# A two-block transformer kernel: queries ahead of keys in latent attention, merge gates and output tiles released earlier

## The chip, the cores and the metric

The kernel runs on one core of one Trainium2 chip. The metric is the device time of one execution in microseconds. Three runs of the kernel before took 3114.63, 3116.35 and 3122.04 us; the median is 3116.35 us.

## What is computed

Two blocks of two layers each work on 256 tokens of width 1024; the first block also has 256 context tokens, which its first layer updates and its second layer only reads. One layer of the first block has, beside norms and modulation, three mixers (latent attention, gated linear attention, neighbourhood attention), a gated merge and a feed-forward part. Cut to what matters here:

```python
def mla_mixer(a_lat, a_ctx, ...):             # latent attention, 8 heads
    qn, qr = mla_queries(a_lat, q_norm_w, w_q_up)      # 64 + 32 features per head
    qr = apply_rope(qr, cos, sin)
    kn, kr, v = mla_keys(a_lat, kv_norm_w, w_kv_up)
    kr = apply_rope(kr, cos, sin)
    ...
    # scores over latent and context keys, softmax, times v

def merge_branches(ya, yb, yc, gates, w_a_o, w_b_o, w_c_o, w_out):
    ga, gb, gc = jnp.split(jax.nn.sigmoid(gates), N_BRANCH, axis=-1)
    return (ga * (ya @ w_a_o) + gb * (yb @ w_b_o) + gc * (yc @ w_c_o)) @ w_out

h = h + g1 * merge_branches(ya, yb, yc, gates, w_a_o, w_b_o, w_c_o, w_out)
```

`gates` is part of the normed input times `w_in`, so it does not depend on the three mixers; `ya`, `yb` and `yc` are their outputs.

## The kernel before, in words

Every product is made of three matmuls (L566 to L568, in `three`): a float32 operand is split into a high part and a low part, and high times high, high times low and low times high are added up in PSUM. Weights come in panels of up to 1 MB. A panel takes this way: SyncE issues its load into one of 3 `raw` buffers (`load_raw`), ScalarE copies it to one of 3 `whi` buffers (L534, in `split_act`, which first waits until the panel three before has been used), VectorE (first five eighths) and GpSimd (the rest) subtract to `wlo` (L543, `split_lo`), and TensorE opens the panel (`open_panel`) when all three are done. When TensorE has used a panel it adds one to `panel_used`. Each engine's program is written out by hand in the order of its instructions, with `step(p)` at the places where it splits the panel two ahead. A stage of the network opens on an engine with `stage(...)` (L574), which waits until all four engines have ended the stage before.

Latent attention (`("mla", l)`, L950 on TensorE). Eight heads; per head `mla_heads` (L1021) projects the keys into bank 7 (6 matmuls of 512 columns) and then the queries into bank 6 (9 matmuls; 512 columns in layer 0, 256 in layer 1, because there the context has no queries). VectorE's `heads` (L2301) waits for both (`qk_done`, L638), scales the keys into `kt` (L2306) and the queries into `qt` (L2307); then TensorE's `mla_rot` (L1043, the matmul L1045) rotates `qt` and VectorE's `rope` (L2271 to L2274) finishes it. GpSimd copies the shared rotary keys `kr` into `kt` (L2752). The next head is prepared at the second item of a head (`prep` on TensorE, `hook` on VectorE); an item is one head and one tile of 128 queries, four a head in layer 0, two in layer 1. Items go through scores (L1064), maximum (L2156), exponential (L1633), transposes (L870), copies (L1644) and the product with the values (L880). In layer 0 the modulation vectors are computed between the items (L770, L759, `mod_vectors` L2042); they share bank 7 with the keys, so TensorE waits for them from head 2 on before it projects a head's keys. The key weights are panel p0 + 5 and the query weights panels p0 + 4 (heads 0 to 3) and p0 + 6 (heads 4 to 7).

Merge (`("merge", l)`, L1322). When the neighbourhood attention has ended, ScalarE copies the 12 tiles of mixer outputs `y` to `yh` (L1870) and VectorE subtracts to `yl` (L2474). TensorE waits for the stage and for the last `yl`, and then loops over 8 output tiles: three gates (24 matmuls each, from `xh`, `xl`, into banks 0 to 2) and three branches (12 matmuls each, from `yh`, `yl`, into banks 3 to 5), from three panels a turn. ScalarE makes the sigmoids (L1880, L1883), VectorE the products and the sum `mf` (L2482 to L2490), which adds one to `merged`. In layer 0 the tiles are 512 columns wide (latent and context tokens), in layer 1 256.

Output (`("out", l)`, L1350). ScalarE waits for all 8 `mf` and for all panels of the merge (L1889), copies `mf` to `xh` (L1891), VectorE subtracts to `xl` (L2497), and TensorE waits for the last `xl` and multiplies with four panels of `w_out`, two tiles of 24 matmuls each (`generic_f`, L822). `three` can also wait for each `xl` by itself, when it is given `fresh`; the norms use this.

Waits of the kernel before that the change touches:

```python
# TensorE, merge, ahead of the loop
stage(pe, "pe", tg, ("na", l))
pe.wait_ge(*dve_done.at((tg, "yl")))
# TensorE, output
stage(pe, "pe", tg, ("merge", l))
pe.wait_ge(*dve_done.at((tg, "ml")))
# ScalarE, output
stage(act, "act", tg, ("merge", l))
act.wait_ge(merged, 8 * (l + 1))
act.wait_ge(panel_used, base[tg])
```

## Time and profile before

| what | value |
|---|---|
| median of the runs | 3116.35 us |
| profiled execution, its own time | 3119.45 us |
| span of its profile | 3117.7 us |
| busy: TensorE, weight loads | 90%, 80% |
| busy: VectorE, ScalarE, GpSimd | 44%, 39%, 36% |
| mean granted clock of TensorE | 0.951 |
| moved by DMA | 413.54 MB, mean 133 GB/s |
| latent attention, heads, layer 0 and 1 | about 124 to 275 us, 1309 to 1390 us |
| merge, layer 0 and 1 | about 598 to 807 us, 1627 to 1742 us |
| output, layer 0 and 1 | about 811 to 860 us, 1745 to 1774 us |

All times in the trace count from the start of the span. A line of the timeline gives start, duration, engine, line of the program, operation, tiles and shape, count of merged instructions, and in brackets how long the engine had been idle before and what released it. In the rows PE is TensorE, DVE VectorE, ACT ScalarE, POOL GpSimd and SPq the queue of SyncE. A clock of 1.00 is 2.4 GHz and one of 0.50 is 1.2 GHz. The duration of one matmul overlaps with the next one, so that the distance of the starts tells the pace.

### The profile page before, as it was taken

To read this page: it belongs to the slowest core of one execution; us is meant where nothing else is said; L and a number is where in the kernel's file an instruction comes from. 1 tells how busy PE (TensorE), PEld (TensorE's weight loads), DVE (VectorE), ACT (ScalarE), POOL (GpSimd) and SP (SyncE) were. 2 spreads that over 40 slices of the span, in tenths; PEclk is the share of its full clock that TensorE was granted. 3 is DMA by queue.
4 is the path that set the end of the run, shared out by engine and by line. 5 is a ranking of instruction groups with operands and counts; after the bars stand their busy time and mean duration, and the time that the engine had idled before them with its cause. 6 is when DMAs were issued, how large, how long until landed. Compare 5 with 4: busy or idle time off the path is not lost. (4 is left out here: it accounts for less than half of the span.)

```text
span 3117.7 us, 52810 instructions
## 1 busy us (share of the span) xinstructions
PE 2812.8 (90%) x20541; PEld 2502.8 (80%) x20541; DVE 1359.5 (44%) x2405; ACT 1217.7 (39%) x1791; POOL 1117.6 (36%) x457
## 2 busy tenths in 40 slices
PE   6789879799889999888789899899889999988998
PEld 4557667588779999566679799899779989977898
DVE  2443533332343433444434543534564353456433
ACT  2322223333244444422345444444444444444443
POOL 0101020132235565111214455354425555632453
PEclk8899989899989999998999999999999999989999
DMA  5454034533336666211415566465225646622563
GB/s 173 131 180 147 14 83 127 156 91 104 94 109 192 188 194 191 83 29 41 88 48 152 164 197 189 141 198 165 95 82 162 188 138 197 190 84 68 149 186 97
DMA packets 570660, 413.54 MB, mean 133 GB/s; under 512 B 36566, under 2 KB 548252, under 8 KB 570524
## 3 DMA queue, kind: packets, MB, share of 16 engines
q1 hardware_dynamic: 570524, 411.69, 44.6%
q8 instruction: 91, 1.49, 0.2%
q14 instruction: 45, 0.37, 0.0%
HBM read 410.58 MB, written 2.88 MB: 133 GB/s over the span
## 5 line engine op out<-in xcount | busy, mean ns | idle before, releaser
L543 POOL TENSOR_TENSOR wlo<-raw,whi 128x768 fp32r<-128x768 f32 (+2 forms) x353 | 1020.3, 2894 | 1701.6 <-ACT whi L534 1701.2
L566 PE MATMUL psum<-xh_n,whi 128*128 128x256 f32 (+1 forms) x3208 | 932.3, 291 | 79.6 <-DVE rtmp L2612 21.7
L567 PE MATMUL psum<-xl_n,whi 128*128 128x256 f32 (+1 forms) x3208 | 915.1, 285 | 0.0
L568 PE MATMUL psum<-xh_n,wlo 128*128 128x256 f32 (+1 forms) x3208 | 914.7, 285 | 0.0
L543 DVE TENSOR_TENSOR wlo<-raw,whi 128x1280 fp32r<-128x1280 f32 (+2 forms) x353 | 531.2, 1505 | 665.3 <-ACT whi L534 665.1
L534 ACT ACTIVATE whi<-raw 128x2048 fp32r<-128x2048 f32 (+2 forms) x353 | 643.2, 1823 | 396.0 <-PE psum L925 171.8
L566 PEld LDWEIGHTS psum<-xh_n,whi 128*128 128x128 f32 x3208 | 615.4, 192 | 114.4 <-issue 57.7
L568 PEld LDWEIGHTS psum<-xh_n,wlo 128*128 128x128 f32 x3208 | 617.3, 192 | 5.5
L567 PEld LDWEIGHTS psum<-xl_n,whi 128*128 128x128 f32 x3208 | 616.4, 192 | 4.7
L923 PE MATMUL psum<-hidh,whi 128*128 128x256 f32 x1232 | 344.0, 279 | 7.0 <-issue 7.0
L925 PE MATMUL psum<-hidh,wlo 128*128 128x256 f32 x1232 | 343.6, 279 | 0.0
L924 PE MATMUL psum<-hidl,whi 128*128 128x256 f32 x1232 | 343.6, 279 | 0.0
L923 PEld LDWEIGHTS psum<-hidh,whi 128*128 128x128 f32 x1232 | 234.1, 190 | 7.5 <-issue 7.5
L925 PEld LDWEIGHTS psum<-hidh,wlo 128*128 128x128 f32 x1232 | 234.7, 191 | 0.0
L924 PEld LDWEIGHTS psum<-hidl,whi 128*128 128x128 f32 x1232 | 234.1, 190 | 0.0
L1653 ACT ACTIVATE sg<-psum 128x256 f32<-128x256 f32 x154 | 59.2, 385 | 420.5 <-PE psum L568 420.4
L2201 DVE TENSOR_TENSOR hidf<-sg,psum 128x256 f32<-128x256 f32 x154 | 64.8, 421 | 259.9 <-ACT sg L1653 259.7
L566 PE MATMUL psum<-xh,whi 128*128 128x512 f32 (+1 forms) x360 | 146.1, 406 | 23.2 <-ACT whi L534 19.9
L567 PE MATMUL psum<-xl,whi 128*128 128x512 f32 (+1 forms) x360 | 143.3, 398 | 0.0
L568 PE MATMUL psum<-xh,wlo 128*128 128x512 f32 (+1 forms) x360 | 142.8, 397 | 0.0
L566 PEld LDWEIGHTS psum<-xh,whi 128*128 128x128 f32 (+1 forms) x360 | 68.9, 191 | 44.5 <-issue 19.0
L2203 DVE TENSOR_TENSOR hidl<-hidf,hidh 128x256 fp32r<-128x256 f32 x154 | 70.6, 458 | 74.6 <-ACT hidh L1655 74.6
(337 smaller groups left out, 3804.3 us busy)
## 6 DMA issues: line engine op xcount, KB each, us to landing
raw<-in_ffn_w_in SPq DMA_DIRECT2D x176, 512.0 KB
raw<-in_w_in SPq DMA_DIRECT2D x136, 512.0 KB
raw<-in_w_ffn_in SPq DMA_DIRECT2D x132, 512.0 KB
raw<-in_w_mod SPq DMA_DIRECT2D x96, 512.0 KB
raw<-in_ffn_w_out SPq DMA_DIRECT2D x88, 512.0 KB
raw<-in_w_ffn_out SPq DMA_DIRECT2D x66, 512.0 KB
raw<-in_w_out SPq DMA_DIRECT2D x32, 512.0 KB
raw<-in_w_a_o SPq DMA_DIRECT2D x16, 256.0 KB
```

Source lines behind the costliest of these rows:

```text
L534: act.activation(whi[slot][:, 0:size], raw[r % 3][:, 0:size], ACT.Copy).then_inc(hi_ready, 1)
L543: eng.tensor_tensor(wlo[slot][:, c0:c1], raw[raw_at[p0] % 3][:, c0:c1], whi[slot][:, c0:c1].bitcast(F32), ALU.subtract).then_inc(sem_, 1)
L566: pe.matmul(dst, sh, mh, start=start and n == 0, stop=False, skip_group_check=True)
L567: pe.matmul(dst, sh, ml, start=False, stop=False, skip_group_check=True)
L568: last = pe.matmul(dst, sl, mh, start=False, stop=n == len(pairs) - 1, skip_group_check=True)
L923: pe.matmul(dst, hi[:, w0:w0 + P], hidh[:, s_, j, :], start=False, stop=False, skip_group_check=True)
L924: pe.matmul(dst, hi[:, w0:w0 + P], hidl[:, s_, j, :], start=False, stop=False, skip_group_check=True)
L925: m = pe.matmul(dst, lo[:, w0:w0 + P], hidh[:, s_, j, :], start=False, stop=False, skip_group_check=True)
L1653: act.activation(sg[:, c, :], bank[4 + c][:, 0:S], ACT.Silu).then_inc(silu_done, 1)
L2201: dve.tensor_tensor(hidf[:, c, :], sg[:, c, :], bank[4 + c][:, S:2 * S], ALU.mult).then_inc(hid_done, 1)
L2203: dve.tensor_tensor(hidl[:, s_, c, :], hidf[:, c, :], hidh[:, s_, c, :].bitcast(F32), ALU.subtract).then_inc(hid_lo, 1)
```

## The change

It makes three edits. (1) In latent attention a head's queries are projected before its keys, on TensorE and in VectorE's copies; `qt` gets its own signal (`"mm q"`), and the panels of the last head are released together by the last key matmul. (2) TensorE no longer opens the merge with a stage and with the wait for `yl`; it waits for `yl` ahead of the first branch in each turn. (3) The output stage has no stage waits; ScalarE converts tiles 0 to 6 of `mf` once seven are merged and the last merge's second panel is used, and tile 7 when it is merged; VectorE signals each `xl`, and TensorE's first output tile waits for them one by one.

```diff
         def qk_done(eng, l, hd):
-            if hd % 4 == 3:
-                eng.wait_ge(panel_used, base["mla", l] + (5 if hd == 3 else 7))
+            if hd == HEADS - 1:
+                eng.wait_ge(panel_used, base["mla", l] + 7)
             else:
                 eng.wait_ge(*pe_done.at((("mla", l), "qk", hd)))
...
-                    if hd >= 2 and l == 0:
-                        pe.wait_ge(*dve_done.at(("mod", "vectors", 8 + 3 * (hd - 1) - 1)))
-                    v = [w_[:, 0:2048].rearrange("p (k n) -> p k n", k=2)[:, :, P * hd:P * hd + 64] for w_ in (whi[(p0 + 5) % 3], wlo[(p0 + 5) % 3])]
-                    m = three(pe, bank[7][0:64, :], [(v[0][:, k, :], v[1][:, k, :], kvh[:, k, :], kvl[:, k, :]) for k in range(2)])
-                    if hd == HEADS - 1:
-                        m.then_inc(panel_used, 1)
                     if hd % 4 == 0:
                         open_panel(pe, p0 + 4 + hd // 2)
                     if hd == 0:
                         pe.wait_ge(*act_done.at(((tg, "q"), "row")))
                         pe.wait_ge(*dve_done.at(((tg, "q"), "lo", 1)))
                     m = proj_f(p0 + 4 + hd // 4 * 2, slice(0, TM), 384, QH * (hd % 4), QH, 3, qdh, qdl, bank[6][0:QH, 0:TM])
-                    if hd % 4 == 3:
+                    if hd == 3:
                         m.then_inc(panel_used, 1)
+                    else:
+                        m.then_inc(*pe_done.tick((tg, "mm q", hd)))
+                    if hd >= 2 and l == 0:
+                        pe.wait_ge(*dve_done.at(("mod", "vectors", 8 + 3 * (hd - 1) - 1)))
+                    v = [w_[:, 0:2048].rearrange("p (k n) -> p k n", k=2)[:, :, P * hd:P * hd + 64] for w_ in (whi[(p0 + 5) % 3], wlo[(p0 + 5) % 3])]
+                    m = three(pe, bank[7][0:64, :], [(v[0][:, k, :], v[1][:, k, :], kvh[:, k, :], kvl[:, k, :]) for k in range(2)])
+                    if hd == HEADS - 1:
+                        m.then_inc(panel_used, 2)
                     else:
                         m.then_inc(*pe_done.tick((tg, "qk", hd)))
...
                 tg = ("merge", l)
                 p0 = base["merge", l]
-                stage(pe, "pe", tg, ("na", l))
-                pe.wait_ge(*dve_done.at((tg, "yl")))
                 m0 = 8 * l
...
                     pe.wait_ge(merged, it + m0)
+                    pe.wait_ge(*dve_done.at((tg, "yl")))
                     branch(1024, 3, 0, hi, lo)
...
                 tg = ("out", l)
-                stage(pe, "pe", tg, ("merge", l))
-                pe.wait_ge(*dve_done.at((tg, "ml")))
                 g = 0
                 for j in range(4):
-                    g = generic_f(tg, base[tg] + j, [(0, P), (P, P)], 8, 256, slice(0, TM), xh, xl, g)
+                    g = generic_f(tg, base[tg] + j, [(0, P), (P, P)], 8, 256, slice(0, TM), xh, xl, g, fresh=None if j else tg)
...
                 tg = ("out", l)
-                stage(act, "act", tg, ("merge", l))
-                act.wait_ge(merged, 8 * (l + 1))
-                act.wait_ge(panel_used, base[tg])
+                act.wait_ge(panel_used, base[tg] - 1)
                 for k in range(8):
+                    if k in (0, 7):
+                        act.wait_ge(merged, 8 * l + (8 if k else 7))
                     act.activation(xh[:, k, 0:TM], mf[:, k, 0:TM], ACT.Copy).then_inc(*act_done.tick((tg, "mh", k)))
...
                 def heads(hd):
+                    if hd == 3:
+                        dve.wait_ge(panel_used, p0 + 5)
+                    else:
+                        dve.wait_ge(*pe_done.at((tg, "mm q", hd)))
+                    if hd == 0:
+                        dve.wait_ge(*act_done.at(((tg, "q"), "row")))
+                    dve.tensor_tensor(qt[0:QH, hd % 2, 0:TM], bank[6][0:QH, 0:TM], stat[0:QH, 0:TM], ALU.mult).then_inc(*dve_done.tick((tg, "q", hd)))
                     qk_done(dve, l, hd)
                     if hd == 0:
-                        for name in ("kv", "q"):
-                            dve.wait_ge(*act_done.at(((tg, name), "row")))
+                        dve.wait_ge(*act_done.at(((tg, "kv"), "row")))
                     dve.tensor_tensor(kt[0:64, hd % 2, :], bank[7][0:64, :], stat2[0:64, :], ALU.mult).then_inc(*dve_done.tick((tg, "kt", hd)))
-                    dve.tensor_tensor(qt[0:QH, hd % 2, 0:TM], bank[6][0:QH, 0:TM], stat[0:QH, 0:TM], ALU.mult).then_inc(*dve_done.tick((tg, "q", hd)))
...
                 tg = ("out", l)
-                stage(dve, "dve", tg, ("merge", l))
                 for k in range(8):
                     dve.wait_ge(*act_done.at((tg, "mh", k)))
                     dve.tensor_tensor(xl[:, k, c], mf[:, k, c], xh[:, k, c].bitcast(F32), ALU.subtract
-                                      ).then_inc(*dve_done.tick((tg, "ml") if k == 7 else None))
+                                      ).then_inc(*dve_done.tick((tg, "lo", k)))
+                dve_done.mark((tg, "ml"))
```

## Rows read from the trace of the kernel before

**Rows 1.** The page, part 1: busy time, share and instructions of each engine.
```profile
PE 2812.8 (90%) x20541; PEld 2502.8 (80%) x20541; DVE 1359.5 (44%) x2405; ACT 1217.7 (39%) x1791; POOL 1117.6 (36%) x457
```

**Rows 2.** The waits of PE, whole span: us in total, times, longest us.
```profile
PE psum L1045 <- DVE qt L2307: 19.8, 16, 1.4
...
PE psum L566 <- DVE yl L2474: 5.7, 1, 5.7
...
PE psum L566 <- DVE mod L2042: 2.1, 6, 0.3
```

**Rows 3.** Timeline, latent attention of layer 0, one head's preparation after its projections.
```profile
188.77 0.68 DVE L2306 TENSOR_TENSOR kt<-psum,stat 64x512 f32<-64x512 f32 x1 [3.83 <-PE psum L568]
...
189.38 0.67 DVE L2307 TENSOR_TENSOR qt<-psum,stat 96x512 f32<-96x512 f32 x1
...
190.10 0.67 PE L1045 MATMUL psum<-qt,cst 96*96 96x256 f32 x2 [1.37 <-DVE qt L2307]
...
190.88 0.42 DVE L2271 TENSOR_TENSOR rt<-psum,cst 32x256 f32<-32x256 f32 x1 [0.83 <-PE psum L1045]
```

**Rows 4.** Timeline, the same in latent attention of layer 1.
```profile
1325.87 0.68 DVE L2306 TENSOR_TENSOR kt<-psum,stat 64x512 f32<-64x512 f32 x1 [2.19 <-PE psum L568]
...
1326.93 0.67 PE L1045 MATMUL psum<-qt,cst 96*96 96x256 f32 x2 [1.10 <-DVE qt L2307]
...
1327.71 0.42 DVE L2271 TENSOR_TENSOR rt<-psum,cst 32x256 f32<-32x256 f32 x1 [0.83 <-PE psum L1045]
```

**Rows 5.** Timeline, end of the neighbourhood attention and front of the merge, layer 0.
```profile
588.57 3.12 POOL L543 TENSOR_TENSOR wlo<-raw,whi 128x768 fp32r<-128x768 f32 x1 [1.63 <-ACT whi L534]
...
596.54 0.95 PE L1274 MATMUL psum<-cst,nytok 128*128 128x128 f32 x4 [0.45 <-DVE nytok L2191]
...
598.97 7.31 DVE L2474 TENSOR_TENSOR yl<-y,yh 128x512 fp32r<-128x512 f32 x12 [2.48 <-ACT yh L1870]
...
606.87 0.77 PE L566 MATMUL psum<-xh,whi 128*128 128x512 f32 x1 [9.38 <-ACT whi L534]
...
610.42 0.39 PE L568 MATMUL psum<-xh,wlo 128*128 128x512 f32 x1
```

**Rows 6.** Timeline, the same place in layer 1.
```profile
1626.33 0.44 PE L1274 MATMUL psum<-cst,nytok 128*128 128x128 f32 x2 [0.45 <-DVE nytok L2191]
...
1627.81 4.11 DVE L2474 TENSOR_TENSOR yl<-y,yh 128x256 fp32r<-128x256 f32 x12 [1.54 <-ACT yh L1870]
```

**Rows 7.** Timeline, end of the merge and front of the output stage, layer 0.
```profile
810.23 0.69 DVE L2490 TENSOR_TENSOR mf<-mt 128x512 f32 x1
811.12 4.27 ACT L1891 ACTIVATE xh<-mf 128x512 fp32r<-128x512 f32 x8 [4.77 <-DVE mf L2490]
811.88 4.90 DVE L2497 TENSOR_TENSOR xl<-mf,xh 128x512 fp32r<-128x512 f32 x8 [0.95 <-ACT xh L1891]
...
817.24 0.77 PE L566 MATMUL psum<-xh,whi 128*128 128x512 f32 x1 [10.53 <-ACT whi L534]
```

**Rows 8.** Timeline, the same place in layer 1.
```profile
1744.32 0.43 DVE L2490 TENSOR_TENSOR mf<-mt 128x256 f32 x1
...
1745.49 2.77 DVE L2497 TENSOR_TENSOR xl_n<-mf,xh_n 128x256 fp32r<-128x256 f32 x8 [0.74 <-ACT xh_n L1891]
...
1748.72 0.55 PE L566 MATMUL psum<-xh_n,whi 128*128 128x256 f32 x1 [8.88 <-DVE xl_n L2497]
...
1753.77 0.34 PE L568 MATMUL psum<-xh_n,wlo 128*128 128x256 f32 x1
```

**Rows 9.** Windows: us, busy and count of PE, PEld, DVE, ACT, POOL; PEclk, DMA share, GB/s.
```profile
596.00:598.00 2.00, 1.04 (x5) 0.55 (x4) 0.28 (x1) 0.47 (x1) 0.00 (x0) 0.69 1.20 290
...
612.00:800.00 188.00, 188.00 (x822) 153.94 (x822) 56.05 (x57) 62.34 (x59) 54.37 (x22) 1.00 0.34 92
...
811.00:813.00 2.00, 0.00 (x0) 0.00 (x0) 1.12 (x2) 1.88 (x4) 0.00 (x0) 0.70 1.03 277
...
1786.00:1788.00 2.00, 1.66 (x9) 1.25 (x9) 1.82 (x5) 1.11 (x3) 0.00 (x0) 1.00 0.00 0
```

## The prediction

> **What bounds the kernel now.** I read the busy times first: TensorE (PE) is busy for 2812.8 us of 3117.7, 90%, no other engine for half of it [rows 1]. So an edit pays if it removes idle time of PE, or if it lets PE start a stage earlier. Next I read what PE waited for, over the whole span. Two kinds of wait belong to the places that the diff touches: the rotation matmul L1045 waits for VectorE's `qt` 16 times, 19.8 us together, and the keys' first matmul waits for `mod` 6 times, 2.1 us [rows 2]. The other places are four gaps of one occurrence each, read from the timelines: the front of the merge loop and of the output stage, in both layers [rows 5 to 8].
>
> **Latent attention.** Today a head runs keys (6 matmuls), queries (9), then on VectorE `kt`, `qt`, and only then the rotation. The head shown of layer 0: `kt` from 188.77, `qt` from 189.38, rotation at 190.10 after 1.37 us of idle PE, first rope operation at 190.88 [rows 3]. After the change the queries are ready 6 matmuls before the keys. Six 512-column matmuls take 6 x 0.229 = 1.4 us (822 matmuls in 188 us [rows 9]), and `qt` with its 0.67 us [rows 3] lies beside them, so the rotation follows the keys without a gap. VectorE then has only `kt` (0.68 us) between the end of the keys and rope. Its chain gets shorter by 190.88 - 188.77 - 0.68 = 1.43 us; PE's by 1.37. Both lead to the next softmax, so the smaller one counts: 8 x 1.37 = 11.0 us. In layer 1 the chain of VectorE loses 1327.71 - 1325.87 - 0.68 = 1.16 us, and PE's idle is 1.10 [rows 4]: 8.8 us. Together that is the 19.8 us of the waits. In layer 0 the wait for `mod` now stands behind the query matmuls (9 x 0.229 = 2.1 us of work, against waits of at most 0.3 us), which takes away the 2.1 us as well. **21.9 us.**
>
> What moves with it: POOL's copy of `kr` still waits for the keys and ends with `kt`; the mod rows, which wait for `kt` of the head, come a whole item later. VectorE gets one new wait, for the queries, at a place where it idles anyway (the `kt` of [rows 3] had been waited for over 3.83 us); `kt`, rope and a weight split stand behind it and PE's rotation waits for it. Panel release: the last key matmul now frees two panels at once, some 9 matmuls later for the keys' panel; the step that reuses it stands behind the whole attention loop, so I cost this at nothing. No DMA is issued anew.
>
> **Merge.** PE stops after the last transposes that start at 596.54 and starts the first gate at 606.87, idle for 9.38 us, released at last by ScalarE, which makes 12 `yh` tiles and a small split first [rows 5]. The gates read only `xh`, `xl` and two weight panels. The second panel's low part was done at 588.57 + 3.12 = 591.7 [rows 5], and banks 0 to 2 have been emptied. So PE can go on at once: 9.4 us. The wait for `yl` moves behind three gates of 24 matmuls, 72 x 0.229 = 16.5 us, that is to about 614; `yl` is complete at 598.97 + 7.31 = 606.3 [rows 5], so that wait costs nothing. What is late next would be ScalarE, but its `yh` tiles and the small split end at 606.8 (PE's wait of today [rows 5]), before the second gate ends at 597.5 + 48 x 0.229 + 1.7 = 610.2. In layer 1 the gap is 5.7 us [rows 2]; `yl` ends at 1627.81 + 4.11 = 1631.9 [rows 6] and the three gates need 72 x 0.115 = 8.3 us from 1626.8, to 1635: covered too. **15.1 us.** This holds only if the clock costs the same. Today PE restarts at the low level: from 606.87 to 610.42 it starts 8 matmuls, 3.55 us instead of 1.83 [rows 5], an extra 1.7 us. In layer 1 the 23 intervals from 1748.72 to 1753.77 take 5.05 us instead of 2.65, an extra 2.4 us [rows 8]. In layer 0 the grant averages 0.69 between 596 and 598 [rows 9], so it fell to 1.2 GHz while the last transposes still ran, before PE was idle. I take both restarts as they are: no gain, no loss. Bounds: the clock stays high, another 1.7 + 2.4 us.
>
> **Output.** Tiles 0 to 6 of `mf` are complete long before the last merge ends; ScalarE now converts seven of them (0.53 us each [rows 7]) while VectorE still builds the eighth. The eighth ends at 810.23 + 0.69 = 810.9; VectorE then does eight `xl` at 0.61 us each (4.90 / 8 [rows 7]), the first ready near 811.7, the last near 816.1. PE starts at 811.8 rather than 817.24 [rows 7]. Its first tile needs 3 matmuls per `xl` part: at the low level the first 8 matmuls take 3.55 us, the other 16 take 16 x 0.229 = 3.7 us, so the tile ends near 819.0; today it ends near 817.24 + 24 x 0.229 + 1.7 = 824.4. Gain 5.4 us. The grant falls between 811 and 813 (0.70 [rows 9]), so low at the start is the likelier case; if it stays high, VectorE's pace decides, the tile ends near 816.8 and the gain is 7.6. In layer 1 `mf` ends at 1744.32 + 0.43, the first `xl` (2.77 / 8 = 0.35 us) near 1745.2, and PE starts there and not at 1748.72 [rows 8]: 3.5 us; at the low level three matmuls take 0.66 us, more than one `xl`, so PE never waits again; clock held: 5.9. The panels for tiles 3 and on are split right behind and come earlier by the same amount. SyncE's loads for block two wait for the last `xl` and are issued some 3 us earlier. **8.9 us.**
>
> A rule speaks against the one-by-one tiles. In the first feed-forward tile after the second norm of layer 1, where PE already waits for each `xl`, PE is busy for 1.66 of 2 us with the clock at 1.00 [rows 9]: short gaps did not bring it down. The Trainium skill, page "TensorE: Matmul & The Clock Gate", section "A second HAM failure mode: psum-queue depth-cycling", says that frequent small idles between groups of matmuls make the clock swing between its two levels. By that rule the first output tile of layer 0 would be low throughout, 24 x 0.444 = 10.7 us, and end at 822.5: 3.5 us of the sum gone, a time of 3074. The trace disagrees so far, and I keep to the row.
>
> **Sum.** 21.9 + 15.1 + 8.9 = 45.9 us. The profiled execution took 3119.45 us (span 3117.7), 3.1 above the median of the runs; its sum would give 3073.6. Against the median, 3116.35 - 45.9 = 3070.5 us. Behind each place PE is again the busy engine and the buffers of weights are full, so an earlier start is passed on.
>
> **Rivals.**
> A: In latent attention another wait takes the place of the rotation's: with PE ahead, the scores wait for `kt` and rope as before. For it: VectorE's chain and PE's idle are almost equal, so both must shrink. Against: both do, by 1.43 and 1.37 us. Nothing of 21.9 us stays: 3092.4.
> B: The clock does not fall at the fronts. All four extras vanish in part: up to 1.7 + 2.4 + 2.2 + 2.4 = 8.7 us more: 3061.8. For it: PE no longer stands still for 9.4 and 5.7 us. Against: the grant of 0.69 before the gap [rows 9].
> C: The merge gives its 15.1 us back: the gates run ahead, then PE waits for ScalarE's next split, as ScalarE's work before it has not become shorter. For it: the wait today ends on ScalarE's `whi` [rows 5]. Against: three gates give 16.5 us of cover in layer 0. 3085.6.
> D, slower: PE starts early but at 1.2 GHz and stays there, as its work in front was light transposes. Place: merge loop of layer 0. Price: 0.444 - 0.229 = 0.215 us a matmul; it decides from 45.9 / 0.215 = 213 matmuls on, two of the eight turns of 108. Over all 864 it is 186 us, so 3070.5 + 186 = 3256. For it: the low grant before the gap. Against: today PE comes from a complete stop and is high after 3.6 us.
> E: The change does nothing because another condition holds the gates. The only others are weights, split by 591.7 [rows 5], and banks; 3116.
>
> **Chances.** Forecast 0.74, A 0.09, B 0.09, C 0.05, D 0.02, E 0.01. The likeliest gives 3070.5. The range goes down past B's 3061.8 by the spread of the runs (3 us) to 3058 and up to C at 3085; A, D and E stay out, 0.12, and I leave the rest for an unforeseen half of A. About 0.3% (9 us) is what a measurement of this kernel can tell from no change. All of forecast, A, B and C are faster by more; D is slower; some part of C and A together with an unseen loss may come near: faster 0.95, same 0.03, slower 0.02.
>
> **What would show it.** Right: L1045 no longer among PE's waits, with rope's first operation 0.7 us after the last key matmul; the first gate matmul right behind the transposes, about 0.1 us later; `gates` and the first `mf` 9 and 6 us closer to the end of the neighbourhood attention; the first output matmul about 5.1 us after the last merge matmul in layer 0 (today 10.5), and ScalarE's seven `xh` before the eighth `mf`. Wrong: a wait of some 1.3 us per head at L1064 or L870 (A), a wait at the fourth panel of the merge on `whi` or `wlo` (C), a grant of 0.5 over more than 4 us of the gates (D), stages behind these places longer than before by what was saved.

## The result, and the profile after the change

The changed kernel takes **3077.37 us** (median of 4 runs, 3065.94 to 3087.2) where the kernel before takes 3119.19 beside it (4 runs, 3114.63 to 3123.0): a ratio of 0.9869, 95% interval 0.9846 to 0.9892, or 41 us less (34 to 48). The forecast was 45.9 us less, 3070.5 us, with a range from 3058 to 3085.

The profiled execution took 3065.94 us, 53.5 less than the one profiled before. That is more than the change did, and the trace says how much more. The two kernels run the same 20541 matmuls in the same order, apart from heads whose queries and keys changed places. So the start of the n-th matmul can be compared, and its difference read where one stage ends and the next begins. In every table below a number is such a difference, in us, gathered within a stage (negative: the changed kernel got ahead). Two of them are read early: merge of layer 1 within its first turn, output of layer 1 within its first 40 matmuls. At the last matmul of each they are -7.2 and -4.3 here.

```
stage                        predicted   measured   (first profile of each)
attention, layer 0              -13.1      -13.3
merge, layer 0                   -9.4       -9.7
output, layer 0                  -5.4       -6.0
second norm, layer 0              0         +2.2
attention, layer 1               -8.8       -6.6
norm behind it, layer 1           0         +0.8
merge, layer 1                   -5.7       -6.6
output, layer 1                  -3.5       -3.6
sum                             -45.9      -42.8
everything else                   0        -10.8
```

The waits of TensorE (PE) in the changed kernel: in us in total, times, longest. The rotation's 19.8 us, `yl` and `mod` of [rows 2] are gone. The two fronts of the output stage stand with 5.0 and 5.4 us instead of 10.53 and 8.88 [rows 7, 8]. Two waits of attention have grown, that of the scores (L1066) to 4.8 us and that of the product with the values (L880) to 5.1.

```profile
PE psum L566 <- DVE xl_n L2500: 5.4, 1, 5.4
PE psum L880 <- ACT prt L1643: 5.1, 3, 2.8
...
PE psum L566 <- DVE xl L2500: 5.0, 1, 5.0
...
PE psum L1066 <- DVE qt L2273: 4.8, 4, 1.6
```

In the kernel before these two (L1064 and L880 there) took 3.3 and 3.2 us:

```profile
PE psum L880 <- ACT prt L1644: 3.2, 3, 1.7
...
PE psum L1064 <- issue: 2.8, 2, 1.4
...
PE psum L1064 <- DVE qt L2274: 0.5, 1, 0.5
```

The timeline of the changed kernel, preparation of one head in layer 1 (start, duration, engine, operation), answers to [rows 4]. The rotation (L1047) follows the last key matmul (L568) after 0.23 us, the pace of PE, and rope (L2270) begins 0.71 us after `kt`, not 1.84.

```profile
1296.40 0.39 PE L568 MATMUL psum<-kvh,wlo 128*64 128x512 f32 x1
...
1296.63 0.59 PE L1047 MATMUL psum<-qt,cst 96*96 96x256 f32 x2
1296.83 0.68 DVE L2311 TENSOR_TENSOR kt<-psum,stat 64x512 f32<-64x512 f32 x1 [0.96 <-PE psum L568]
...
1297.54 0.42 DVE L2270 TENSOR_TENSOR rt<-psum,cst 32x256 f32<-32x256 f32 x1
```

The same view at the front of the merge, layer 0, answers to [rows 5]: the first gate matmul starts 0.41 us behind the start of the last four transposes, and `yl` is made while the gates run.

```profile
583.54 0.66 PE L1276 MATMUL psum<-cst,nytok 128*128 128x128 f32 x4 [0.45 <-DVE nytok L2190]
583.95 0.53 PE L566 MATMUL psum<-xh,whi 128*128 128x512 f32 x1
...
585.67 7.32 DVE L2478 TENSOR_TENSOR yl<-y,yh 128x512 fp32r<-128x512 f32 x12 [2.19 <-ACT yh L1869]
```

And at the front of the output stage, layer 0, three rows for [rows 7], of VectorE, ScalarE and PE. ScalarE converts seven tiles before the last merged tile `mf` exists, and PE's first matmul starts 1.44 us after the operation that makes this last `mf`, not 7.01.

```profile
783.25 3.73 ACT L1890 ACTIVATE xh<-mf 128x512 fp32r<-128x512 f32 x7
```
```profile
787.25 0.69 DVE L2494 TENSOR_TENSOR mf<-mt 128x512 f32 x1
787.86 6.53 DVE L2500 TENSOR_TENSOR xl<-mf,xh 128x512 fp32r<-128x512 f32 x8
```
```profile
788.69 0.77 PE L566 MATMUL psum<-xh,whi 128*128 128x512 f32 x1 [4.97 <-DVE xl L2500]
```

Two things in these rows ask for an experiment. The eight `xl` took 6.53 us where they took 4.90 before [rows 7]. And attention in layer 1 gained 2.2 us less than forecast. Its keys were ready at these times:

```profile
1304.45 0.68 DVE L2311 TENSOR_TENSOR kt<-psum,stat 64x512 f32<-64x512 f32 x1 [0.98 <-PE psum L568]
1312.06 0.68 DVE L2311 TENSOR_TENSOR kt<-psum,stat 64x512 f32<-64x512 f32 x1 [0.97 <-PE psum L568]
1325.33 0.68 DVE L2311 TENSOR_TENSOR kt<-psum,stat 64x512 f32<-64x512 f32 x1 [1.95 <-PE psum L568]
1332.94 0.68 DVE L2311 TENSOR_TENSOR kt<-psum,stat 64x512 f32<-64x512 f32 x1 [0.96 <-PE psum L568]
```

The other intervals are about 1.1 us shorter than before; the one behind head 4 (1312.06 to 1325.33, 13.27 us) is 1.22 longer (12.05 before). There VectorE's middle operation of rope (L2271) takes 1.81 us, while GpSimd, which began 0.27 us earlier, splits a panel of weights:

```profile
1312.78 0.42 DVE L2270 TENSOR_TENSOR rt<-psum,cst 32x256 f32<-32x256 f32 x1
1313.12 1.81 DVE L2271 TENSOR_TENSOR qt<-qt,cst 32x256 f32<-32x256 f32 x1
1314.97 0.42 DVE L2273 TENSOR_TENSOR qt<-qt,rt 32x256 f32<-32x256 f32 x1
1315.42 1.49 DVE L543 TENSOR_TENSOR wlo<-raw,whi 128x1280 fp32r<-128x1280 f32 x1
```
```profile
1312.85 1.81 POOL L543 TENSOR_TENSOR wlo<-raw,whi 128x768 fp32r<-128x768 f32 x1
```

### The profile page after: what moved, and what is told of

Same layout as the page of the kernel before. It is cut to its first block and busy times, and to the rows that moved or that the text cites. A ratio compares the mean times of both kernels' runs of the same rounds, so it can differ in the third digit from the quotient of the medians.

```text
span 3064.1 us, 52810 instructions
## 1 busy us (share of the span) xinstructions
PE 2795.2 (91%) x20541; PEld 2489.6 (81%) x20541; DVE 1368.7 (45%) x2405; ACT 1217.7 (40%) x1791; POOL 1118.0 (36%) x457
## 3 DMA queue, kind: packets, MB, share of 16 engines
q8 instruction: 91, 1.49, 0.2%
## 5 line engine op out<-in xcount | busy, mean ns | idle before, releaser
L566 PE MATMUL psum<-xh_n,whi 128*128 128x256 f32 (+1 forms) x3208 | 930.1, 290 | 73.4 <-DVE rtmp L2616 21.9
L568 PE MATMUL psum<-xh_n,wlo 128*128 128x256 f32 (+1 forms) x3208 | 912.0, 284 | 0.0
L566 PEld LDWEIGHTS psum<-xh_n,whi 128*128 128x128 f32 x3208 | 615.2, 192 | 107.9 <-issue 51.4
L568 PEld LDWEIGHTS psum<-xh_n,wlo 128*128 128x128 f32 x3208 | 616.3, 192 | 5.5
L566 PE MATMUL psum<-xh,whi 128*128 128x512 f32 (+1 forms) x360 | 146.2, 406 | 8.3 <-DVE xl L2500 5.0
L568 PE MATMUL psum<-xh,wlo 128*128 128x512 f32 (+1 forms) x360 | 143.4, 398 | 0.0
L1654 ACT ACTIVATE hidh<-hidf 128x256 fp32r<-128x256 f32 x154 | 64.4, 418 | 89.3 <-DVE hidf L2200 89.3
```

Source lines behind the costliest of these rows:

```text
L566: pe.matmul(dst, sh, mh, start=start and n == 0, stop=False, skip_group_check=True)
L568: last = pe.matmul(dst, sl, mh, start=False, stop=n == len(pairs) - 1, skip_group_check=True)
L1654: act.activation(hidh[:, s_, c, :], hidf[:, c, :], ACT.Copy).then_inc(hid_hi, 1)
```

## The experiments

### The three edits alone, and the whole again

`e1_mla` is the kernel before with the attention edit (here in words):

```
-  keys of the head; then its queries;   DVE: kt, qt, rotation, rope
+  queries of the head; tick "mm q";     DVE: wait "mm q", qt, wait keys, kt, rotation, rope
```

> The attention edit alone (the turned queries and keys one head ahead), the merge and the output as before. By the sum of the prediction: 21.9 us less than the kernel before. By the trace of the whole change, in which the steps of layer 1 came only 5.8 us earlier instead of 8.8: 13.3 + 5.8 = 19.1 us less, and in layer 1 the interval from head 4's keys to head 5's is longer than before (12.05 us there, 13.3 us expected here). If the wait were merely replaced (rival A): 0 us. The merge and the output loops should keep their own gaps before them, 9.38 and 10.53 us in layer 0, as in the kernel before. Since profiled executions of one kernel differ by up to 20 us, the ratio of the rounds and the start differences by stage are both read.

`e2_merge`, with the merge edit:

```
-                stage(pe, "pe", tg, ("na", l))
-                pe.wait_ge(*dve_done.at((tg, "yl")))
...
                    pe.wait_ge(merged, it + m0)
+                    pe.wait_ge(*dve_done.at((tg, "yl")))
```

> The merge edit alone: the fifteenth stage's gate products start before the attention outputs, and their wait stands behind them. By the prediction 15.1 us less than the kernel before (9.4 in layer 0, 5.7 in layer 1); by the trace of the whole change 9.7 + 7.0 = 16.7 us less. By rival C (the merge gives its gain back to the output's wait): 0 to 3 us less, and the gap before the output loop grows above the 10.53 us of before.

`e3_out`, with the output edit:

```
-                pe.wait_ge(*dve_done.at((tg, "ml")))
...
+                    ... generic_f(..., fresh=None if j else tg)
...
-                act.wait_ge(merged, 8 * (l + 1))
...
+                    if k in (0, 7):
+                        act.wait_ge(merged, 8 * l + (8 if k else 7))
```

> The output edit alone: merged tiles split and taken one by one. By the prediction 8.9 us less than the kernel before (5.4 + 3.5); by the trace of the whole change 6.0 + 4.0 less, minus 2.2 us that the norm behind layer 0's output gives back because its sums run at the lower clock: 7.8 us less. If these sums run at the full clock here (eight sums in 7.5 us, not 9.1), the give-back is no part of this edit.

`e4_all_again` is the changed kernel, unaltered.

> The changed kernel again, nothing altered. The first three edits share no instructions, so if nothing of one eats another's gain, their three gains add up to this one's: 19.1 + 16.7 + 7.8 = 43.6 us by the trace of the whole change, 45.9 us by the prediction. Its profile also tells where the spread of its times (3065.9 to 3087.2 us) comes from: my theory is that single feed-forward stages run at a matmul pitch of 0.118 us instead of 0.113 at the same granted clock, 5.5 us or more each, by chance and in both kernels; the rival is that the changed stages differ from one execution to the next, and then the starts within attention, merge and output differ by several us between this profile and the last.

Measured against 3120.86 us for the kernel before (19 runs, 3106.83 to 3131.98):

```
run            median    ratio, 95% interval       us less   by the stages of its profile
e1_mla         3101.10   0.9938 (0.9914-0.9961)      19.3        14.4
e2_merge       3101.75   0.9953 (0.9931-0.9975)      14.7        16.7
e3_out         3111.24   0.9975 (0.9959-0.9992)       7.8         6.6
e4_all_again   3082.94   0.9883 (0.9854-0.9912)      36.5        42.7
```

The three add up to 41.8 us, close to the 36.5 (27 to 46) of the whole beside them and the 41 of the first comparison. The stages below show that no edit eats another's gain. The stages, for these and all later profiles (A attention, M merge, O output, N2 the second norm behind O of layer 0, NA the norm behind A of layer 1; 0 and 1 the layers; against the first profile of before):

```
profile                A0     M0     O0     N2     A1     NA     M1     O1
before, second       -1.8   -0.1    0.1    0.1    0.0    0.0    0.0    0.2
before, third         0.1    0.0    0.0    0.1    0.0    0.0    0.3    0.3
before, fourth        0.0    3.5    0.0    0.1    0.0    0.0    0.3    0.2
changed, first      -13.3   -9.7   -6.0    2.2   -6.6    0.8   -6.6   -3.6
changed, e4         -13.3   -9.7   -6.2    2.2   -6.5    0.8   -6.5   -3.5
changed, e9         -13.3   -9.6   -6.2   -0.2   -7.8    0.9   -6.6   -3.7
changed, e10        -13.3   -9.5   -6.2    2.2   -6.6    0.8   -6.6   -3.4
e1_mla               -8.2    0.4    0.2    0.1   -6.8    0.0   -0.1    0.0
e2_merge              0.0   -9.9   -0.1   -0.1    0.0    0.0   -6.6    0.0
e3_out                0.0    0.0   -6.2    2.2    0.0    0.9   -0.2   -3.3
e5_pool_later        -9.9   -9.6   -6.2    2.2   -9.1    0.0   -6.6   -3.4
e6_yl_first         -13.3    0.2   -5.9   -0.2   -7.7    0.9   -0.1   -3.4
e7_last_xl          -13.3   -9.4    0.1   -0.1   -7.8    1.0   -6.6   -0.7
```

Each edit moves its own columns and no other, but for N2 and NA. Most entries repeat within 0.2 us; the larger part of the runs' spread lies elsewhere (below). M1 and O1 are the two columns that are read early. At the last matmul of the stage M1 is between -6.6 and -7.3 in the seven profiles in which it is gained, and O1 between -4.0 and -4.4 in the seven with the whole output edit; without the edit O1 drifts there by up to 0.9 us.

A0 holds stretches at the lower clock, and they differ between executions. The second profile of before is 1.8 us ahead of the first, mainly because one of them is missing in it; against it the changed kernel gains 11.5 us in A0 and not 13.3. The windows of the first and of the second profile of before:

```profile
197.00:201.00 4.00, 4.00 (x30) 2.98 (x30) 0.92 (x3) 1.05 (x3) 0.00 (x0) 0.57 1.02 337
```
```profile
197.00:201.00 4.00, 4.00 (x36) 2.44 (x34) 1.36 (x5) 1.05 (x3) 0.00 (x0) 1.00 1.00 333
```

Two other entries of A0 are small, -8.2 and -9.9. The windows of e1_mla there (us, then busy time and count of PE, PEld, DVE, ACT and POOL, the granted clock, DMA share, GB/s) show the cause:

```profile
188.00:192.00 4.00, 4.00 (x24) 2.08 (x25) 1.14 (x4) 0.09 (x1) 0.00 (x0) 0.50 1.03 348
192.00:196.00 4.00, 4.00 (x18) 3.40 (x16) 0.67 (x4) 1.05 (x3) 0.00 (x0) 0.50 0.96 319
196.00:200.00 4.00, 4.00 (x24) 1.82 (x23) 1.18 (x3) 0.44 (x1) 0.00 (x0) 0.50 0.07 22
200.00:204.00 4.00, 4.00 (x15) 3.25 (x16) 0.45 (x2) 0.61 (x3) 0.00 (x0) 0.50 0.78 260
204.00:208.00 4.00, 4.00 (x17) 2.40 (x16) 1.88 (x4) 0.00 (x0) 0.60 (x1) 0.92 0.00 0
```

PE is busy all the time, at 1.2 GHz, for 16 us and a little more. In the changed kernel's first profile the clock falls at the same point of the work and is back at 1.00 from 192 us on:

```profile
188.00:192.00 4.00, 4.00 (x28) 2.08 (x28) 1.37 (x5) 0.30 (x1) 0.00 (x0) 0.57 0.96 322
192.00:196.00 4.00, 4.00 (x39) 2.66 (x37) 1.63 (x5) 1.23 (x4) 0.00 (x0) 1.00 1.02 342
```

### What stands behind head 4 and behind the 6.53 us of `xl`

`e5_pool_later` is the changed kernel with two waits more on GpSimd:

```
                     if hd == 4:
+                        pool.wait_ge(*dve_done.at((tg, "qk", 4)))
                         step(p0 + 5)
...
                 for j in range(4):
+                    if j == 0:
+                        pool.wait_ge(*dve_done.at((("out", l), "lo", 7)))
                     step(base["out", l] + j)
```

> The changed kernel, with two waits more on GpSimd: its share of a weight split behind head 4's key copy waits until VectorE has turned that head's queries, and its first split of the output stage waits for VectorE's last split of a merged tile. Theory: in the changed kernel GpSimd's split starts just ahead of a VectorE product with two operands in SBUF, which then stands still until GpSimd is done: head 4's turn in layer 1 takes 1.81 us instead of the 0.41 of its 15 sisters, and one of the eight splits of the output in layer 0 takes 2.31 instead of 0.68. Then here all 16 turns take 0.41 us, all eight splits 0.68 (their sum 4.9 us, not 6.53), the interval from head 4's keys to head 5's in layer 1 is 1.4 to 2.2 us shorter (11.1 to 11.9 us instead of 13.27), and the output of layer 0 comes up to 1.6 us earlier; 2 to 4 us less in all, which the ratio of the rounds can hardly show, so the starts by stage decide. Rival 1: VectorE's own wait (for GpSimd's key copy, or for memory) makes these operations long; then they stay at 1.81 and 2.31 us. Rival 2: the split of GpSimd comes late for the panel it fills, TensorE waits for it, and the kernel gets slower by 1 to 3 us at one of the two places.

The operations behaved as the theory has it. Rope's middle operation, grouped (duration min/median/max), in the changed kernel and then in e5:

```profile
L2271 DVE TENSOR_TENSOR qt<-qt,cst x16: 405/406/1811, 129.9 to 1341.6; 32x256 f32<-32x256 f32 x16
```
```profile
L2271 DVE TENSOR_TENSOR qt<-qt,cst x16: 406/406/418, 131.8 to 1344.4; 32x256 f32<-32x256 f32 x16
```

The eight splits of the output, layer 0, likewise:

```profile
L2500 DVE TENSOR_TENSOR xl<-mf,xh x8: 677/684/2310, 787.9 to 793.7; 128x512 fp32r<-128x512 f32 x8
```
```profile
L2500 DVE TENSOR_TENSOR xl<-mf,xh x8: 683/684/686, 793.4 to 797.6; 128x512 fp32r<-128x512 f32 x8
```

So rival 1 (VectorE waits for something of its own) is out: only GpSimd's start was moved. The interval from head 4's keys to head 5's is 10.70 us, less than the 11.1 to 11.9 expected. In e5 it is GpSimd that stands still. Its split starts 0.1 us behind VectorE's and takes 3.05 us instead of 1.81, and the stage gets shorter all the same: PE does not pay for it (rival 2 is out too).

```profile
1319.43 3.05 POOL L543 TENSOR_TENSOR wlo<-raw,whi 128x768 fp32r<-128x768 f32 x1 [1.35 <-DVE qt L2273]
```

Whoever comes second waits for the whole operation of the first: 0.41 becomes 1.81 us on VectorE, 1.81 becomes 3.05 on GpSimd beside VectorE's 1.49. The Trainium skill, page "SBUF — State Buffer", section "SBUF: two separate sides", says the same: a VectorE operation with two SBUF inputs and a GpSimd operation that reads SBUF contend for an exclusive lock, and the loser blocks. These rows agree.

What the two moves were worth differs. In the table above A1 went to -9.1 us, from -6.6 in three profiles of the changed kernel and -7.8 in the fourth, in e6 and in e7. So the block itself costs 1.3 us, and another 1.2 comes or goes with the clock: e9, where rope's operation takes 1.81 us as well, needs 12.05 us from head 4's keys to head 5's, and the first profile 13.27. The windows behind head 4, first profile and then e9:

```profile
1316.00:1320.00 4.00, 2.02 (x11) 1.49 (x9) 2.72 (x6) 2.33 (x6) 0.00 (x0) 0.76 0.49 144
1320.00:1324.00 4.00, 4.00 (x17) 3.40 (x17) 0.70 (x2) 0.12 (x1) 0.00 (x0) 0.50 0.34 118
1324.00:1328.00 4.00, 4.00 (x21) 2.85 (x20) 2.54 (x5) 0.00 (x0) 0.60 (x1) 0.88 0.00 0
```
```profile
1314.00:1318.00 4.00, 2.02 (x16) 1.66 (x15) 2.51 (x7) 2.44 (x6) 0.00 (x0) 1.00 0.56 159
1318.00:1322.00 4.00, 4.00 (x16) 2.78 (x15) 0.80 (x3) 0.00 (x0) 0.14 (x1) 0.57 0.30 103
1322.00:1326.00 4.00, 3.94 (x24) 2.63 (x22) 3.46 (x9) 1.26 (x3) 0.46 (x1) 1.00 0.01 2
```

In the output, layer 0, the repaired splits bought nothing: O0 is -6.2 as in e4. There PE's own pace covers the block, which my expectation overlooked: its first matmuls run at 1.2 GHz, with a start every 0.43 us and three matmuls for each `xl`, so it gets to the late `xl` only after the block is over. By its four runs e5 is at 0.9883 (0.9865 to 0.9901), the value of e4; 2.6 us can't be told that way, and its own A0 lost 3.4 us to a stretch of some 14 us at the lower clock.

### The waits put back one at a time

`e6_yl_first` is the changed kernel with `yl` waited for ahead of the merge loop:

```
                 m0 = 8 * l
+                pe.wait_ge(*dve_done.at((tg, "yl")))
                 with repeat(pe, 8) as it:
...
                     pe.wait_ge(merged, it + m0)
-                    pe.wait_ge(*dve_done.at((tg, "yl")))
```

> The changed kernel with one wait moved back: TensorE waits for the low parts of the attention outputs ahead of the merge loop, as before, while its waits for the other engines' ends stay removed. Theory: the whole gain of the merge edit is that the gate products run while these low parts are made, so 15.1 (prediction) to 16.7 us (trace) are lost: about 9.4 to 9.7 in layer 0 and 5.7 to 7.0 in layer 1, and the gap of about 9 us before the loop is back. Rival: part of the gain came from the waits for the other engines' ends that the change removed; then a loss of 5 to 10 us only.

The gap in layer 0 is back (9.23 us), M0 and M1 read 0.2 and -0.1: putting this one wait back takes all 16.3 us of the merge, and dropping the wait for the other engines' ends is worth nothing by itself. What that wait would hold back if it alone were put back was not run. The time is 3088.44 us against 3117.26 (11 runs), 0.9902 (0.9882 to 0.9921), 30.5 us less. The stages of its profile sum to 29.5.

```profile
586.32 0.66 PE L1276 MATMUL psum<-cst,nytok 128*128 128x128 f32 x4 [0.45 <-DVE nytok L2190]
596.21 0.76 PE L566 MATMUL psum<-xh,whi 128*128 128x512 f32 x1 [9.23 <-ACT whi L534]
```

`e7_last_xl`, with the last split waited for ahead of the output stage:

```
                 tg = ("out", l)
+                pe.wait_ge(*dve_done.at((tg, "ml")))
                 g = 0
...
-                    ... generic_f(..., fresh=None if j else tg)
+                    ... generic_f(...)
```

> The changed kernel, but the output products wait for the last merged tile's split, as before, while ScalarE still converts seven of the eight tiles inside the merge loop. Theory: TensorE starts behind the eight splits instead of behind the first, 5.7 us later in layer 0 (6.53 us of splits less the first) and 2.4 us in layer 1, and takes its first products without waits between them: 5 to 6 us lost in layer 0 and 2.4 to 3 in layer 1, 7.5 to 9 in all, nearly the whole gain of the output edit. Rival: the early conversion carries half of the gain, and 4 us are lost.

```profile
789.86 6.50 DVE L2501 TENSOR_TENSOR xl<-mf,xh 128x512 fp32r<-128x512 f32 x8
```
```profile
796.42 0.79 PE L566 MATMUL psum<-xh,whi 128*128 128x512 f32 x1 [10.69 <-DVE xl L2501]
```

PE idles for 10.69 us again. O0 reads +0.1 instead of -6.2, O1 -0.7 instead of -3.5: 9.1 us lost, 2.2 of them regained in N2; expected were 7.5 to 9 in all. The early conversion alone is worth nothing in layer 0, where GpSimd's block eats what it saves (6.50 us of splits, not 4.90), and 0.7 in layer 1. Its six runs say 3091.04 us, 0.9919 (0.9895 to 0.9943), 25.2 us less, where the stages of its profile sum to 36.8; that difference is of the kind discussed next.

### Where the spread comes from

Five profiles of unaltered kernels. `e8_before_again`, `e11_before_third` and `e12_before_fourth` are the kernel before, `e9_all_third` and `e10_all_fourth` the changed one.

> The kernel before, nothing altered, for a second profile of it. Theory: attention, merge and output start and end as in its first profile within 0.5 us of each other, except where the lower clock lasts longer; what else differs are feed-forward stages at a pitch of 0.118 us instead of 0.113, 4 to 7 us each, in other places than the last one. Rival: the last feed-forward stage runs at 0.118 us again, and so it is the kernel's, and the change cured it.

> The changed kernel, nothing altered, for one more profile. Open is whether the longer stretch at the lower clock in layer 0's attention (17 us behind 188 us in two of the six profiles that hold the attention edit, 4 us in the others and in all four without the edit) comes with the edit or by chance. If it comes with the edit in one execution of three, about one of this and the next profile shows it, 3.5 to 4 us later behind head 5, and none of the two of the kernel before does. If it is chance of the chip, it shows in those as well. Feed-forward stages at 0.118 us a matmul: one of seven or so, in any place, by my theory; all of them 0.113 by none.

> As for the third profile of the changed kernel: the same question, one more execution. Head 4's turn in layer 1 takes 1.81 us again, and the norm behind layer 0's output has its sums at the lower clock again (9.1 us for eight, not 7.5), since both follow from the order of the work and not from chance.

> The kernel before, nothing altered, for its third profile. If the long stretch at the lower clock in layer 0's attention is chance of the chip, it shows in some of these as well, some 4 us later behind head 5; if it belongs to the attention edit, not. The sums behind layer 0's output run in 7.5 us.

> The kernel before, its fourth profile, with the same question as the third. With it there are four of each kernel: the mean of their spans should differ by 40 to 48 us, and less those of their feed-forward stages that run at 0.118 us a matmul the spans of each kernel should lie within 5 us of one another.

Times: 3112.3, 3123.05 and 3129.64 us of before, 3063.61 and 3072.79 of the changed kernel. Behind the changed stages the first profile of before lost another 9.6 us against the changed kernel's, 5.4 of it in its last feed-forward stage (193.1 us from its first matmul to its last, against 187.6), the rest in small pieces. The 5.4 are this (all L566 matmuls of 30 us; the changed kernel's first profile, then before's, both at the same work and mostly at full clock):

```profile
L566 PE MATMUL psum<-xh_n,whi x61: 276/276/276, 2906.8 to 2932.7; 128*128 128x256 f32 x61
```
```profile
L566 PE MATMUL psum<-xh_n,whi x64: 281/281/387, 2903.1 to 2928.3; 128*128 128x256 f32 x64
```

Each matmul takes 5 ns more, and they start 0.118 us apart instead of 0.113. This lasts for a whole feed-forward stage (5.5 to 7 us more) and then is gone. Over 14 profiles 19 of 98 such stages ran so: 1, 1, 2 and 3 of seven in the four of before, 0, 1, 1 and 1 in the four of the changed kernel, 9 of 42 in the others, and each of the seven places at least twice. In e8 the last stage ran at 0.113 and the fourth at 0.118, so the rival, that the last stage of before is slow by its nature and the change cured it, is out.

The second source is how long a stretch at 1.2 GHz lasts at the same point of the same work. In A0, at 188 us and later, it is some 3.4 us in most profiles, but some 17 in e1 and some 14 in e5; against the -13.3 of the changed kernel that cost 5.1 us and 3.4 us. Ahead of the merge it is some 14 us in before's first profile and 31 in its fourth, which cost 3.5 (in the table under M0). A stage of e5 behind 2702 us, which no edit touches, lost some 7 us with the clock at 0.51 for 20 us. As long stretches appeared in the kernel before too, they aren't the attention edit's alone. In A0 the long stretch was seen in two of eight profiles with that edit and in none of six without, which doesn't settle whether the edit makes it more frequent there; e9 and e10 did not show it.

Two more expectations failed. e10's held that the slow sums of N2 follow from the order of the work; e10 has them, and e9, the same kernel, has not. e12's put the difference of the mean spans at 40 to 48 us; it is 52.5. The four profiles of before hold seven slow feed-forward stages and those of the changed kernel three. At 5.5 to 7 us each that is 5.5 to 7 us of the difference of the means, and takes it to about 46 (an estimate). The same expectation had the spans of each kernel within 5 us of one another once the slow stages are taken out; that fails too, as the long stretches at the lower clock have to be taken out as well.

What stays open: the four profiled executions of the changed kernel took 3063.6 to 3072.8 us, mean 3068.6; its eight runs without a profile 3069.2 to 3093.9, mean 3082.0. Before shows no such difference (profiled 3112.3 to 3129.6, all others 3106.8 to 3132.0). Runs without a profile leave no trace, so it is not known whether they had more slow feed-forward stages or something of the change that four profiles missed.

## Why the prediction was right, and where its terms were off

The forecast was 45.9 us; the stages say 42.8, the two comparisons 41 and 36.5 (27 to 46). The mechanism held in each of the six places. That the sum comes so close is in part luck: about 5 us were lost in layer 1's attention and in two norms, and about 2 gained elsewhere, mostly in layer 0's output and layer 1's merge, and the sum has neither.

**Attention, layer 0.** 11.0 + 2.1 = 13.1 forecast, 13.3 measured in six profiles against the first of before, but 11.5 against its second: the clock alone moves this stage by more than the forecast missed it. Rival A (another wait takes the rotation's place) fell: the rotation's 16 waits took 19.8 us, and the waits of the scores and of the product with the values grew by 1.5 and 1.9 (by 0.7 and 0.2 in e5).

**Attention, layer 1: the term that was mis-sized.** "VectorE then has only `kt` (0.68 us) between the end of the keys and rope", and with it 8.8 us. This took rope at its usual length. It overlooked that a shorter chain of VectorE moves rope onto GpSimd's weight split, which waits for the same keys: 0.41 us became 1.81 at one head, 1.2 more went with the clock behind it, and 6.6 us were left (7.8 without the fall of the clock). With GpSimd moved away (e5) it is 9.1, so the term was right for a rope of the usual length. The prediction went through VectorE's queue and PE's; of POOL it said only that its copy "still waits for the keys and ends with `kt`". The split behind that copy was not followed. In the kernel before the two already met, for 0.68 us instead of 0.41.

**Merge.** 9.4 forecast and 9.4 to 9.9 measured in layer 0; 5.7 and 6.6 in layer 1. "I take both restarts as they are" missed 0.8 of the 0.9 us there. Before, PE came back from a stop and ran 25 matmuls at the lower clock (1632.46 to 1637.74); now it ran 17 (1594.34 to 1597.93). 8 x (0.213 - 0.113) = 0.8 us. That is rival B in part, in one of four places. Rival C (the gain goes to a wait for the panels) fell: in layer 0 PE waits for nothing from the first gate to the end of the loop, and with the merge edit alone (e2) the gap ahead of the output is 10.56 us, as before. In layer 1 seven short waits for GpSimd's split, in the later turns, grew from 2.4 to 3.7 us; the stage's gain at its last matmul is 7.2 us all the same. Rival D fell with the granted clock at 0.57 from 584 to 588 us and at 1.00 from 588 to the end of the loop.

**Output.** 5.4 forecast and 5.9 to 6.2 measured, 3.5 and 3.3 to 3.7. Layer 0's first tile ended 8.1 us after `mf` was complete, as worked out (810.9 to 819.0 there, 787.9 to 796.0 here), though its inputs were not as forecast: the splits took 6.53 us instead of 4.90, and PE's low clock hid it. The rest of the difference is that the first tile of before ended later than I took it. The prediction also priced the case of a clock that is low for the whole tile, 10.7 us. It was low for the first part only: the matmuls that start from 789.25 to 791.81 take 0.63 us each, those from 792.58 on 0.40, while VectorE's splits run on until 794.39. That does not test the rule of the Trainium skill, page "TensorE: Matmul & The Clock Gate", section "A second HAM failure mode: psum-queue depth-cycling", which the prediction set beside it. The rule speaks of small idles that make the clock swing, not of a clock that stays low. And PE had no idle in this tile: behind the first matmul the starts lie 0.43 and then 0.23 us apart, without a wait for any later `xl`.

**"An earlier start is passed on": the step that failed.** It was passed on only in part, in two norms. Behind layer 0's output the sums of squares (L593) ran in part at 1.2 GHz in three of the four profiles of the changed kernel, in e3 and in e5, and 2.2 us were given back. The windows of the changed kernel's first profile, and the same of e9, the fourth, where nothing was given back:

```profile
834.00:838.00 4.00, 2.14 (x5) 0.82 (x4) 1.12 (x4) 1.63 (x3) 0.00 (x0) 0.85 0.00 0
838.00:842.00 4.00, 4.00 (x8) 1.40 (x6) 0.00 (x0) 1.88 (x4) 0.00 (x0) 0.72 0.02 4
```
```profile
834.00:838.00 4.00, 2.14 (x6) 0.68 (x4) 1.12 (x4) 1.78 (x3) 0.00 (x0) 1.00 0.00 0
838.00:842.00 4.00, 4.00 (x10) 1.48 (x10) 0.00 (x0) 2.62 (x5) 0.00 (x0) 1.00 0.02 4
```

It never showed without the output edit (before four times, e1, e2), nor with half of it (e7), nor in e6, which has the whole edit. In the norm behind layer 1's attention 0.8 to 1.0 us went the same way, in the four profiles of the changed kernel, in e3, e6 and e7, and not in e5, e1, e2 or before. No run shows what decides it. The last output matmul of layer 0 starts at 833.9 us in the first profile and at 834.0 in e9, and the clock fell in one and not in the other. So the cause stays open. The prediction passed everything on because "PE is again the busy engine" behind each place; in the norm behind layer 0's output PE is busy for 2.14 of 4 us, and the two norms cost 3.0 us.

## What to carry to other kernels

When a wait is shortened, look at what every engine that was released by the same event does next, GpSimd too: operations that used to miss one another may now meet. Where one is a VectorE product of two tiles in SBUF and the other GpSimd's subtraction, as here, the later one stands still. Move the one on which nobody waits, by a wait on the other. And to judge a change of one per cent, compare the starts of the n-th matmul stage by stage: here most stages repeated within 0.2 us while whole executions of one kernel differed by 25. Take more than one profile of each kernel: a stretch at the lower clock that comes or goes moved a stage by 1.8 to 5 us.

## What was not expected of the hardware

- Whole feed-forward stages run at 281 ns a matmul instead of 276, starts 0.118 us apart instead of 0.113, at a full granted clock: 19 of 98 stages, in either kernel, 5.5 to 7 us each. No run here shows a cause.
- A stretch at the lower clock lasts some 3.4 us in one execution and some 14 or 17 in another, or is missing, with the same work in front of it and PE busy throughout (e1: 188 to 204 us at 0.50; before at 197 us: 0.57 in the first profile, 1.00 in the second).
- A VectorE product of 32x256, 0.41 us alone, took 1.81 us beside a GpSimd subtraction of 128x768 that began 0.27 us earlier; that subtraction took 1.81 us there and 3.05 in e5, where a VectorE subtraction of 128x1280 had begun 0.1 us earlier.
